# A relative-position bias built by a broadcast write and a strided read instead of reversing products

## What is computed

```python
def dilated_attention(q, k, v, rel_bias):
    for (w, d) in DIL_PATTERNS:                     # (128, 1), (512, 4), (2048, 16)
        rel = d * jnp.arange(-half, half + 1)
        patterns.append((rel, rel_bias[t5_bucket(rel)].T))
...
            kpos = qpos[:, None] + rel[None, :]
            valid = (kpos >= 0) & (kpos < S)
            s = s + bias.astype(jnp.float32)[None, :, None, :]
            s = jnp.where(valid[None, None], s, -jnp.inf)
...
    # the patterns' outputs are merged by their softmax denominators
```

## Time and profile before

| | |
|---|---|
| median of the runs | 1656.06 us (1655.53 to 1656.3, 3 runs) |
| span of the profiled execution | 1652.8 us |
| TensorE busy | 1595.9 us |
| VectorE, ScalarE, GpSimd busy | 1120.9, 921.6, 132.4 us |
| moved by DMA | 301.09 MB, mean 182 GB/s |

### The profile page before, as it was taken

How to read it: one execution, slowest core, us unless ns; L and a number is a source line. 1 busy time by engine, 2 the same in 40 slices (tenths; PEclk the granted TensorE clock), 3 DMA queues, 4 the chain that set the end, 5 groups by cost and what they waited for, 6 DMA issues and landing times. The chain is left out here.

```text
span 1652.8 us, 31090 instructions
## 1 busy us (share of the span) xinstructions
PE 1595.9 (97%) x12890; PEld 1465.8 (89%) x12890; DVE 1120.9 (68%) x1763; ACT 921.6 (56%) x1467; POOL 132.4 (8%) x106
## 2 busy tenths in 40 slices
PE   5999989999999999989999999999999999999999
PEld 2987578999999999966899999878999998799999
DVE  2799667645566655897754556777887567788873
ACT  3444656645365444647554445766666467676662
POOL 0230000112001100300012100000011000001110
PEclk8999999999999999999999999999999999999999
DMA  9433666656546555435466553314555633235553
GB/s 386 161 147 142 255 230 232 228 223 233 194 167 222 200 187 200 154 128 217 172 216 201 187 198 130 117 56 144 194 200 187 216 118 118 78 132 203 206 190 120
DMA packets 45164, 301.09 MB, mean 182 GB/s; under 512 B 5232, under 2 KB 7504, under 8 KB 11744
## 3 DMA queue, kind: packets, MB, share of 16 engines
q1 hardware_dynamic: 44304, 297.44, 50.6%
q0 software_dynamic: 288, 0.92, 0.1%
q10 hardware_dynamic: 432, 0.75, 0.1%
HBM read 298.02 MB, written 1.06 MB: 181 GB/s over the span
## 5 line engine op out<-in xcount | busy, mean ns | idle before, releaser
L2018 DVE TENSOR_TENSOR wl<-raw,wh 128x1040 fp32r<-128x1040 f32 (+1 forms) x472 | 567.3, 1241 | 313.1 <-ACT wh L1771 220.6
L1771 ACT ACTIVATE wh<-raw 128x1040 fp32r<-128x1040 f32 (+1 forms) x472 | 465.5, 1030 | 182.7 <-PE bank L1560 95.2
L1555 PE MATMUL bank<-hx_hi,wh 128*128 128x256 f32 x1856 | 522.6, 282 | 6.0 <-ACT hx_hi L1771 3.8
L1560 PE MATMUL bank<-hx_lo,wh 128*128 128x256 f32 x1856 | 516.7, 278 | 0.0
L1558 PE MATMUL bank<-hx_hi,wl 128*128 128x256 f32 x1856 | 514.6, 277 | 0.2 <-DVE wl L2018 0.2
L1555 PEld LDWEIGHTS bank<-hx_hi,wh 128*128 128x128 f32 x1856 | 349.1, 188 | 12.8 <-issue 11.8
L1558 PEld LDWEIGHTS bank<-hx_hi,wl 128*128 128x128 f32 x1856 | 349.0, 188 | 4.3 <-issue 3.6
L1560 PEld LDWEIGHTS bank<-hx_lo,wh 128*128 128x128 f32 x1856 | 348.9, 188 | 1.2 <-DVE hx_lo L2011 0.4
L1558 PE MATMUL bank<-hid_hi,wl 128*128 128x256 f32 x912 | 252.2, 277 | 1.1 <-DVE wl L2018 1.1
L1555 PE MATMUL bank<-hid_hi,wh 128*128 128x256 f32 x912 | 252.4, 277 | 0.1
L1560 PE MATMUL bank<-hid_lo,wh 128*128 128x256 f32 x912 | 252.0, 276 | 0.0
(11 more groups left out here) (219 smaller groups left out, 1909.1 us busy)
## 6 DMA issues: line engine op xcount, KB each, us to landing
raw<-in_wts SPq DMA_DIRECT2D x208, 1032.0 KB, 4.9
raw<-in_wts SPq DMA_DIRECT2D x50, 1024.0 KB, 6.5
raw<-in_wts SPq DMA_DIRECT2D x20, 776.0 KB, 4.2
raw<-in_wts SPq DMA_DIRECT2D x4, 584.0 KB, 4.2
tmp<-tscr SPq DMA_DIRECT2D x16, 128.0 KB, 3.9
raw<-in_wts SPq DMA_DIRECT2D x2, 648.0 KB, 3.9
xTc<-in_ctxT SPq DMA_DIRECT2D x1, 1024.0 KB, 10.8
xTx<-in_xT SPq DMA_DIRECT2D x1, 1024.0 KB, 8.1
```

Source lines behind the costliest of these rows:

```text
L1555: pe.matmul(out, block(f, M.wh, w0 + k, ncols, c, m), x_hi, start=first and k == 0 and o == 0, stop=False, skip_group_check=True)
L1560: ins = pe.matmul(out, block(f, M.wh, w0 + k, ncols, c, m), x_lo, start=False, stop=last and k == nk - 1, skip_group_check=True)
L1771: return act.activation(out, in_, func, bias=bias, scale=scale)
L2018: tt(M.wl[k][:, cols], M.raw[r][:, cols], M.wh[k][:, cols].bitcast(F32), ALU.subtract).then_inc(*on.inc(lo))
```

## The change

The scratch tensor grows from (8, 512) to (8, 128, 512). One transfer writes the table of 8 partitions into it 128 times. Row p of a head's 128 rows is then read from element 255 - 128 qt - p on: a step of 511 elements from one partition to the next goes one row on and one element back. So two transfers, one for each half of the queries, put the whole bias of all 8 heads straight into `M.bias`, in round 2. The temporaries, the reversing products, the copies by ScalarE and the constant `flip` go. SP now waits ahead of the reads for the scratch write and for the former users of the memory of `M.bias` (`b1_free`), in place of waits by ScalarE.

```diff
-    sq = np.concatenate([c[k] for k in ("ident", "ones", "bones", "swap1", "swap2", "flip")], axis=1)
+    sq = np.concatenate([c[k] for k in ("ident", "ones", "bones", "swap1", "swap2")], axis=1)
...
-    def bias_read(h):
-        b = tmps.get()
+    def load_bias():
         t_in = [ev("bias_in", 16), ev("bias_in", 16)]
-        step("bias_in", h=h, b=b, free=flat([tscr_free, b.free, small.get("turn")]), t_in=t_in)
-
-        def turn():
-            o = banks.get()
-            t, x = ev("mm"), ev("bias")
-            step("bias", h=h, b=b, o=o, o_free=o.free, b1_free=b1_free, ready=t_in, t=t, x=x)
-            tmps.give(b, t)
-            small["turn"] = t
-            banks.give(o, x)
-            t_bias[:] = [x]
-        return turn
-
-    turns = []
+        step("bias_in", free=flat([tscr_free, b1_free]), t_in=t_in)
+        t_bias[:] = t_in
 
     def bias_step(i):
-        if i < 2:
-            (load_tables, tables)[i]()
-            return
-        if turns:
-            turns.pop(0)()
-        if i < 10:
-            turns.append(bias_read(i - 2))
+        if i < 3:
+            (load_tables, tables, load_bias)[i]()
...
-    def bias(b, o, o_free, ready, t, **_):
-        on.wait_ge(ready, o_free)
-        mm(o.t[:, :], M.flip, b.t[:, :], True, True).then_inc(*on.inc(t))
...
-    def bias(h, o, b1_free, t, x, **_):
-        on.wait_ge(t, b1_free)
-        fn(M.bias[:, h, :], o.t[:, :], ACT.Copy).then_inc(*on.inc(x))
...
     def tables(lc, t_l, t_w, **_):
         on.wait_ge(t_l)
-        sp.dma_start(io["tscr"][:, :], lc.t[0:8, :]).then_inc(*on.inc(t_w, 16))
-
-    def bias_in(h, b, free, t_in, **_):
+        sp.dma_start(io["tscr"], lc.t[0:8, :].unsqueeze(1).to_broadcast([8, P, 512])).then_inc(*on.inc(t_w, 16))
+
+    def bias_in(free, t_in):
         on.wait_ge(free)
         for qt in range(2):
-            src = bass.AP(io["tscr"].tensor, h * 512 + P - P * qt, [[1, P], [1, T]])
-            sp.dma_start(b.t[:, qt * T:qt * T + T], src).then_inc(*on.inc(t_in[qt], 16))
+            src = bass.AP(io["tscr"].tensor, 255 - P * qt, [[511, P], [512 * P, 8], [1, T]])
+            sp.dma_start(M.bias[:, :, qt * T:qt * T + T], src).then_inc(*on.inc(t_in[qt], 16))
...
-    io["tscr"] = nc.dram_tensor("tscr", (8, 512), F32, kind="Internal").ap()
+    io["tscr"] = nc.dram_tensor("tscr", (8, P, 512), F32, kind="Internal").ap()
```

More of the change, by code:

```diff
@@ L90, in shape_constants @@
     c["swap2"] = j2
-    c["flip"] = np.eye(P)[::-1]
-    sq = np.concatenate([c[k] for k in ("ident", "ones", "bones", "swap1", "swap2", "flip")], axis=1)
+    sq = np.concatenate([c[k] for k in ("ident", "ones", "bones", "swap1", "swap2")], axis=1)
     t = np.arange(T)
@@ L205, in __init__ @@
         vec = sb("vec", [P, NV])
-        cst = sb("cst", [P, 6 * P])
+        cst = sb("cst", [P, 5 * P])
         self.vec, self.cst = vec, cst
@@ L219, in __init__ @@
         b1_off = cur[0]
-        self.ident, self.ones, self.bones, self.swap1, self.swap2, self.flip = (
-            cst[:, P * i:P * i + P] for i in range(6))
+        self.ident, self.ones, self.bones, self.swap1, self.swap2 = (
+            cst[:, P * i:P * i + P] for i in range(5))
         self.V = lambda k: vec[:, VT[k][0]:VT[k][0] + VT[k][1]]
@@ L1751, in tensor_program @@
                 "hn2": hn2, "qn2": qn2, "poolproj": poolproj, "conv1": conv1, "conv2": conv2, "sc1": sc1, "turn1": turn1,
-                "val1": val1, "sub1": sub1, "tables": tables, "bias": bias, "lora2": lora2, "mla_v": mla_v,
+                "val1": val1, "sub1": sub1, "tables": tables, "lora2": lora2, "mla_v": mla_v,
                 "mla_k1": mla_k1, "mla_k2": mla_k2, "sc2": sc2, "turn2": turn2, "val2": val2})
@@ L1997, in scalar_program @@
                 "stsplit": stsplit, "silu": silu, "hidsplit": hidsplit, "lambdas": lambdas, "tables": tables,
-                "bias": bias, "lora1": lora1, "lora2": lora2, "mla_v": mla_v, "mla_k1": mla_k1, "mla_k2": mla_k2,
+                "lora1": lora1, "lora2": lora2, "mla_v": mla_v, "mla_k1": mla_k1, "mla_k2": mla_k2,
                 "exp2": exp2, "turn2": turn2, "val2": val2, "tconv": tconv, "gate2": gate2})
```

## The result

The changed kernel takes 1672.83 us (median of 4 runs, 1671.76 to 1674.09) against 1655.8 us for the kernel before in the same session: a ratio of 1.0107, 95% interval 1.0093 to 1.0121. It is slower, by 17.0 us. The profiled execution spans 1670.5 us against 1652.8, 17.7 us more; the prediction said 1670.6 for the span and 1674 for the median.

The account below looks back on a forecast made before the run. TensorE, busy for 97% of the span, was taken as the bound. Waits of 20.1 and 3.9 us plus 1.5 for the clock, less 7.7 gained, made 17.8 us longer: 1674 us, range 1647 to 1688, likeliest case alone 1663 to 1690.

Parts of the forecast that it names:

- The gain, 7.5 us on TensorE: Layer 1's first feed-forward: eight reversing products leave TensorE, 6.9 us, with the first one's 0.66 us wait for its transfer.
- Rival 3: The change frees nothing because the eight products only filled gaps: 1656 us with a quick write, chance 0.02.
- The 0.15 us at the opening: Opening transfers: constants shrink from 384 to 320 KB, saving 0.15 us at most.
- The write, 38.8 us: Scratch write on SP's queue: 2.10 MB from partitions 0 to 7 at 54 GB/s takes 38.8 us, ending at 861.7.
- The row of 54 GB/s: Profile stretch around the load of the 16 KB log-count table into the same eight partitions, taken as the write's rate.
- rival 1: The scratch write is quick, 9.9 us on half of the engines, and nothing waits: 1648.4 us, chance 0.24.
- The wait for up7, 20.1 us: TensorE near 847 us: up7's weights queue behind the write, so it starts at 867.0 instead of 846.9.
- The reads, 9.9 us: Two 1 MB bias reads behind up8, at half the weight rate: 9.9 us, from 866.7 to 876.6.
- a second wait of 3.9 us: TensorE near 878 us: up9, needed at 875.7, lands behind the reads at 879.6, a wait of 3.9 us.
- The clock, 1.5 us: Behind TensorE's 20 us wait, one 3.3 us stretch at the lower granted clock, 0.56, costs 1.5 us.
- Who stands behind the write: SP's queue: up7 behind the write in the same rings, up9 and up10 behind SP's wait; 8 us of longer write free.
- The deciding point: Below 18.8 us for the write nothing waits; each microsecond more costs one; at 26.5 us gain and loss cancel.

Follow-up runs that it names:

- kernel with the spread eight partitions: The changed kernel with the table made on 32 partitions and the write taking every fourth one, 0 to 28: 1646.69 us, against 1652.83 for the kernel before.
- The last experiment: The changed kernel with 23 extra products of 128x512 in TensorE's queue just ahead of up7: 1671.76 us, ratio 1.0100 to the kernel before.
- The kernel with late reads: The changed kernel with the bias reads, and SP's wait for the write, moved from round 2 of the feed-forward to round 8: 1672.77 us.
- 128-partition kernel: The changed kernel with the table made on 128 partitions, each written 8 times, the same 2.10 MB: ratio 0.9951 to the kernel before.

## Why the prediction held, point by point

**The gain, 7.5 us on TensorE.** Right. In the kernel with the spread eight partitions, where nothing waits, the gate product of round 1 comes at 833.3 us instead of 833.6 and the last at 928.8 instead of 936.8: 7.7 us. Rival 3, a change that frees nothing, is out. The 0.15 us at the opening were never seen: by 819 us the kernels of this study lie between 0.8 us ahead of the kernel before and 1.4 behind.

**The write, 38.8 us.** The step that carried the forecast, and the right end of the range: 42.3 us. As far as it rests on rows, the number was right by luck. The row of 54 GB/s, 4 GB/s too fast, is a mean over 0.34 us of which the second part moved nothing:

```profile
810.27:810.42 0.15, 0.15 (x3) 0.15 (x3) 0.15 (x2) 0.15 (x1) 0.00 (x0) 1.00 0.52 123
810.42:810.61 0.19, 0.19 (x4) 0.17 (x2) 0.19 (x2) 0.19 (x1) 0.00 (x0) 1.00 0.01 0
```

And the old write's eight packets, out of the same partitions, took 0.084 us each in the trace of before, as quick as those of the spread kernel. So the low rates of those short stretches come largely from packets that start one after the other, as rival 1 held, and not from the 0.30 us per packet that made the long write slow. No row of before shows that cause. The prediction had it from a page alone: the Trainium skill (SBUF — State Buffer, "Door 1") gives two ports of about 27 GB/s for these partitions, and its estimate of 38.6 us was 3.7 short, since 49.6 GB/s over the write is 25 for each of the two. Rival 1 fell on this number alone, and the spread kernel shows it alive: with the write at 10.6 us the time is 1646.7, where the rival said 1648.4.

**The wait for up7, 20.1 us.** Right in place and mechanism, 2.7 short. TensorE reached up7 at 846.92 + 0.11, as forecast (846.9), started at 868.6 and lacked the second half's rest for another 1.2 us: 22.8 in all. The 3 us come from the longer write (3.5 us longer, begun at 822.3 instead of 822.9).

**The reads, 9.9 us, and a second wait of 3.9 us.** The reads' packets took 9.8 us (866.1 to 875.9), and up9 was split at 878.9, against 879.6 forecast for its landing. Even that agreement is chance: 9.9 was half of the weight rate, and the reads had weights of up8 and up9 beside them; with little beside them they take 6.8 us (last section). But nobody waited. The forecast let TensorE run up7 and up8 at full pace behind the first wait; it started 1.6 us later, at the lower clock, and so came to up9 late enough. This term was wrong by all of itself: it left out that a longer first wait also puts off the need for the next piece.

**The clock, 1.5 us.** Right in kind; 17.4 + 7.7 - 22.8 leaves 2.3 us for it, since the lower clock lasted 5.9 us into the work instead of 3.3. The last experiment gives 1.7.

**The sum.** 17.8 forecast, 17.7 in the span. It is closer than its terms, which is luck too: 2.7 more on up7, 0.8 on the clock, 3.9 less on the reads; 17.4 in all, as the stage has it. The range was not the sum of its own terms: 1663 is (6.5 and 4 off), but 12 and 13 more would be 1699 and not 1690.

**Who stands behind the write.** The prediction named two: up7 in the rings, and up9 and up10 behind SP's wait. The kernel with late reads shows that SP's wait, the second, costs nothing, and leaves the first. The temporary held by the write was missing from the list.

**The deciding point.** "Each microsecond more costs one" was too mild. With 16 partitions the write takes 20.8 us, 2.0 beyond the 18.8; the forecast's rule leaves 5.7 of the 7.7 us of gain, and the kernel is 2.6 us faster than the one before (1652.5, a single run, to 1655.13), 3.2 us by the gate products. Waits of TensorE in it:

```profile
PE bank L1537 <- ACT wh L1749: 1.3, 1, 1.3
PE bank L1540 <- DVE wl L1992: 1.0, 1, 1.0
```

A stretch of the same kernel right behind them has the clock at 0.52:

```profile
852.00:855.30 3.30, 3.30 (x18) 3.30 (x17) 2.62 (x3) 1.84 (x3) 1.87 (x1) 0.52 1.11 372
```

So even waits of 2.3 us in all are followed by 3.3 us at 0.52, up to 1.6 us of lost clock.

## What to carry to other kernels

Price a transfer by where its partitions lie, not by its bytes: 2.1 MB out of eight neighbouring partitions took 42 us, and the same from every fourth partition 10.6. Ahead of weights in the same rings such a transfer delays them by its whole length beyond the idle time of the queue, so read off when the next piece is really needed. A change that trades engine work for a transfer should be tried again with the transfer spread before it is given up; here that turned 1.1% slower into 0.5% faster.

## What was not expected of the hardware

- **An issue can block.** SP's issue of a 1 MB load takes 0.33 us; behind the slow write up7's took 5.57 us. SP's queue in the changed kernel, from 830 to 835 us:

```profile
830.72 5.57 SPq L2321 DMA_DIRECT2D raw<-in_wts  x1
```

  Up8's took 4.6 more, up9's 4.5 where it followed directly (late reads). With the spread eight partitions up7's issue took 0.34 us, and so it did with 16 neighbours, whose packets are as slow as the changed kernel's. What tells them apart is how much of the write was left, an estimate from its start, its end and the time of the issue: some 100 packets on each engine in the changed kernel, about 38 in the other two. Where ScalarE issues the slow write, SP's issue of up7 takes 0.33 us. So what blocks goes with the packets that still stand in SP's own rings; which buffer fills stays open.
- **Half a weight piece comes early.** Behind the slow write the eight engines that have no part in it finish their half of up7 at 840.4, the others at about 867.1. The piece counts as landed with the last.
- **Reads at a step of 511 are quick.** With little beside them, the 2.1 MB came in 6.8 us of packets (128-partition kernel), some 310 GB/s, where the old reads of one head's 2 KB ran near 90.
